# Attention of a decoder trunk on one Trainium2 core: one q/k/v projection per tile from strided views of h, and units that follow it by two steps

## What is computed

```
DILATION_PATTERNS = ((128, 1), (512, 4), (2048, 16))       # window, dilation
qkv = (x @ w_in).reshape(b, s, 3, N_GROUPS, ATTN_HEADS, ATTN_HEAD_DIM)
for g, (window, dilation) in enumerate(DILATION_PATTERNS):
    q = rms_norm(qkv[:, :, 0, g], q_gain[g]) * (ATTN_HEAD_DIM ** -0.5)
    k = rms_norm(qkv[:, :, 1, g], k_gain[g])
    o, l = dilated_window_attention(q, k, qkv[:, :, 2, g], rel_bias[:, g], window, dilation)
wts = jax.nn.softmax(jnp.stack(lses), axis=0)
y = jnp.einsum('gbsh,gbshe->bshe', wts, jnp.stack(outs))
```

## Time and profile before

| | before |
|---|---|
| median of 3 runs | 3387.8 us (3387.46 to 3390.41) |
| the profiled execution | 3383.74 us, its span 3382.0 us |
| granted clock, mean | 0.978 |
| busy: PE, PEld, DVE, ACT, POOL | 94%, 79%, 39%, 33%, 24% |
| attention, from first projection to last unit | 34.9 to 1301.6 us |

### The profile page before, as it was taken

One profiled execution on the slowest core, in us unless ns is written; L12 is line 12 of the kernel. 1 busy time (PEld: TensorE's weight loads), 2 busy tenths in 40 slices (PEclk: granted clock), 3 DMA queues, 4 the chain that ended last, 5 costly groups with the idle time before them and its releaser, 6 DMA issues. The chain is left out here.

```text
span 3382.0 us, 48256 instructions
## 1 busy us (share of the span) xinstructions
PE 3192.3 (94%) x17466; PEld 2669.5 (79%) x17466; DVE 1334.0 (39%) x3725; ACT 1102.1 (33%) x3002; POOL 825.2 (24%) x598
## 2 busy tenths in 40 slices
PE   4999999999999995999999999899877999999999
PEld 3888888888888883878888888678655788888887
DVE  6445454555555554341313133541064431313131
ACT  4555555555555553321111112210244211111020
POOL 3332333333233320212222122112111122222221
PEclk9999999999999995999999999999998999999999
DMA  2112121211112114111111111111201111111112
GB/s 98 36 40 59 41 58 40 61 49 50 52 45 53 47 32 150 50 44 47 48 50 44 50 50 45 38 44 50 81 26 57 44 50 44 50 50 44 50 45 80
DMA packets 89904, 177.01 MB, mean 52 GB/s; under 512 B 25515, under 2 KB 55870, under 8 KB 89662
## 3 DMA queue, kind: packets, MB, share of 16 engines
q1 hardware_dynamic: 87358, 169.63, 16.1%
q10 hardware_dynamic: 2304, 4.20, 0.3%
HBM read 160.67 MB, written 13.12 MB: 51 GB/s over the span
## 5 line engine op out<-in xcount | busy, mean ns | idle before, releaser
L69 PE MATMUL ps_qk<-w_hi,attn_hT_hi 128*128 128x256 f32 x1536 | 437.4, 285 | 23.3 <-DVE attn_hT_lo L213 9.7
L915 POOL TENSOR_TENSOR first_w_lo<-first_raw,first_w_hi 128x1024 fp32r<-128x1024 f32 x96 | 231.7, 2414 | 900.8 <-ACT first_w_hi L911 900.8
L70 PE MATMUL ps_qk<-w_lo,attn_hT_hi 128*128 128x256 f32 x1536 | 436.1, 284 | 0.0
L71 PE MATMUL ps_qk<-w_hi,attn_hT_lo 128*128 128x256 f32 x1536 | 436.1, 284 | 0.0
L857 POOL TENSOR_TENSOR w_lo<-raw,w_hi 128x384 fp32r<-128x384 f32 x192 | 194.6, 1015 | 701.9 <-ACT w_hi L602 701.9
L915 POOL TENSOR_TENSOR second_w_lo<-second_raw,second_w_hi 128x1024 fp32r<-128x1024 f32 x72 | 172.2, 2391 | 630.0 <-ACT second_w_hi L911 630.0
L69 PEld LDWEIGHTS ps_qk<-w_hi,attn_hT_hi 128*128 128x128 f32 x1536 | 294.1, 191 | 27.6 <-issue 13.3
L635 ACT ACTIVATE prob<-ps_s,neg_max 128x128 f32<-128x128 f32 (+1 forms) x384 | 156.6, 413 | 439.7 <-DVE neg_max L726 439.7
L70 PEld LDWEIGHTS ps_qk<-w_lo,attn_hT_hi 128*128 128x128 f32 x1536 | 294.7, 192 | 0.4
L71 PEld LDWEIGHTS ps_qk<-w_hi,attn_hT_lo 128*128 128x128 f32 x1536 | 294.9, 192 | 0.0
L69 PE MATMUL first_ps<-first_hid_hi,first_w_hi 128*128 128x512 f32 x640 | 255.4, 399 | 32.7 <-DVE first_hid_lo L1239 32.7
(11 more groups left out here) (276 smaller groups left out, 6853.9 us busy)
## 6 DMA issues: line engine op xcount, KB each, us to landing
raw<-in_wqkv SPq DMA_DIRECT2D x192, 192.0 KB, 2.3
first_raw<-in_w SPq DMA_DIRECT2D x64, 512.0 KB, 3.4
second_raw<-in_w SPq DMA_DIRECT2D x64, 512.0 KB, 3.4
w_bc<-share_dram SPq DMA_DIRECT2D x48, 256.0 KB, 4.2
first_raw<-in_vo_pieces SPq DMA_DIRECT2D x16, 512.0 KB, 3.5
bias<-bias_dram SPq DMA_DIRECT2D x16, 256.0 KB, 3.6
yT_dram<-o_g SPq DMA_DIRECT2D x8, 512.0 KB, 3.1
first_raw<-in_attn_wo SPq DMA_DIRECT2D x8, 512.0 KB, 3.5
```

The source lines that it names most:

```text
L69: pe.matmul(out, a_hi, b_hi, start=first, stop=False)
L70: pe.matmul(out, a_hi, b_lo, start=False, stop=False)
L71: return pe.matmul(out, a_lo, b_hi, start=False, stop=last)
L915: pool.tensor_tensor(self.lo[:, n % 2, :], self.raw[:, n % self.RAW, :], self.hi[:, n % 2, :].bitcast(F32), ALU.subtract).then_inc(self.lo ...
```

## The change

The q/k/v projection of a tile becomes one stream: 24 matmuls of 384 columns, `hT` stationary. The 128 tokens of a tile are now those of a unit, taken from h by a view: contiguous in group 0, every 4th token in group 1, every 8th in group 2 (`tile_view`). In group 2 a tile holds two residues modulo 16, and the bias masks the pairs that mix them (`bias_onehot`). q, k and v come out in the order that the units need, v with tokens in partitions, so the permuting copies, `vT` and its transposes are gone; `v_hi` holds 8 tiles. A unit starts two steps after its tile (`LAG = 2`), its weighted values two steps after its scores; the merge and the store follow about one superstep earlier, and supersteps run to 25.

```diff
+UNIT_STRIDE = (1, 4, 8)
...
+def tile_view(ap, g, u):
     if g == 0:
-        return ap
+        return ap[:, u * P:(u + 1) * P]
     if g == 1:
+        return ap.rearrange("p (n i r) -> p r n i", n=2, r=4)[:, u // 2, u % 2, :]
+    return ap.rearrange("p (m u) -> p u m", u=TT)[:, u, :]
...
-LAST_SUPER = SECTIONS + 2
+LAST_SUPER = SECTIONS + 1
+LAG = 2
...
-                U = T - TT
+                U = T - LAG
...
-                        mm = split_matmul(pe, ps_qk[j % 2][:, 0:2 * P],
-                                          hT_hi[:, k, j * P:(j + 1) * P], hT_lo[:, k, j * P:(j + 1) * P],
-                                          w_hi[:, par, k, 0:2 * P], w_lo[:, par, k, 0:2 * P], k == 0, k == KT - 1)
+                        mm = split_matmul(pe, ps_qkv[j % 2][:, 0:W3],
+                                          tile_view(hT_hi[:, k, :], st % NG, j), tile_view(hT_lo[:, k, :], st % NG, j),
+                                          w_hi[:, par, k, :], w_lo[:, par, k, :], k == 0, k == KT - 1)
...
+                if st < SECTIONS:
+                    if st >= 1 or j >= 2:
+                        pe.wait_ge(qkn_done, T - 1)
+                        pe.wait_ge(v_lo_done, T - 1)
+                    project(0, KT).then_inc(qkv_mm, 1)
+                if has_unit(st, j, 2):
+                    sec, u = unit(st, j, 2)
...
+                    for b in range(first, 2):
+                        slot = u - 1 + b
+                        mm = split_matmul(pe, ps_o[:, 0:2 * P], v_hi[:, slot, :], v_lo[:, slot, :],
+                                          pT_hi[:, b, :], pT_lo[:, b, :], b == first, b == 1)
...
-                    if st >= 1:
-                        if j == 0:
-                            pe.wait_ge(vT_done, 2 * N)
-                        mm = pe.transpose(ps_t[:, 2 * P:3 * P], vT[:, (st - 1) % 2, j * P:(j + 1) * P], ident[:])
...
-                    for k in range(2 * (j % 4), 2 * (j % 4) + 2):
-                        mm = split_matmul(pe, ps_v[:], w_hi[:, par, k, 2 * P:3 * P], w_lo[:, par, k, 2 * P:3 * P],
-                                          hT_hi[:, k, half * HALF:(half + 1) * HALF],
-                                          hT_lo[:, k, half * HALF:(half + 1) * HALF], k == 0, k == KT - 1)
...
-                    act.activation(sq[:], ps_qk[j % 2][:, 0:2 * P], ACT.Square).then_inc(squared, 1)
+                    act.activation(sq[:], ps_qkv[j % 2][:, 0:2 * P], ACT.Square).then_inc(squared, 1)
+                    act.copy(v_hi[:, j, :], ps_qkv[j % 2][:, 2 * P:W3]).then_inc(v_hi_done, 1)
...
-                if st >= 4 and (st - 4) % NG == 0:
-                    pair = (st - 4) // NG + 2 * i
+                if st >= 3 and (st - 3) % NG == 0:
+                    pair = (st - 3) // NG + 2 * i
```

More of the change, by code:

```diff
@@ L54, in bias_onehot @@
         band = window // dilation
+        mixed = dilation // UNIT_STRIDE[g]
         for x in range(BIAS_LEN):
-            step = x - (P - 1)
-            if step < 0 or step > band:
+            step, other = divmod(x - (P - 1), mixed)
+            if step < 0 or step > band or other:
                 out[g, REL_BUCKETS, x] = 1.0
@@ L349, in attention_phase @@
         gains = sb("gains", [P, 2, NG])
[L350 to L353, removed]
+        qk_hi = sb("qk_hi", [P, 2, SEQ], F32R)
+        qk_lo = sb("qk_lo", [P, 2, SEQ], F32R)
+        v_hi = sb("v_hi", [P, TT, P], F32R)
+        v_lo = sb("v_lo", [P, TT, P], F32R)
         sq = sb("sq", [P, 2 * P])
@@ L366, in attention_phase @@
         stat_rows = sb("stat_rows", [4 * TT, P])
-        vT, w_bc, prob = buffers.vT, buffers.w_bc, buffers.prob
+        w_bc, prob = buffers.w_bc, buffers.prob
         o_raw = [buffers.o_g0, total[:].rearrange("p (o t) -> p o t", o=1), buffers.o_g2]
         ring = sb("ring", [P, HALF])
[L370 to L379, removed]
+        compact = sb("compact", [P, NG, 2, 2, TT])
+        top = sb("top", [P, 2, TT])
+        diff = sb("diff", [P, NG, 2, TT])
+        grown = sb("grown", [P, NG, 2, TT])
+        part = sb("part", [P, NG, 2, TT])
+        den = sb("den", [P, 2, TT])
+        share = sb("share", [P, NG, 2, TT])
+        ps_qkv = [ps(f"ps_qkv{i}", [P, HALF]) for i in range(2)]
         ps_t = ps("ps_t", [P, HALF])
@@ L429, in _, with load_bias @@
             sp.dma_start(gains[HD:P, 1, :], k_gain).then_inc(gains_in, 16)
+            def load_bias(g, pair):
+                base = (g * HEADS + 2 * pair) * BIAS_LEN
+                width = 2 * P if g < 2 else P
+                sp.dma_start(bias[g][:], bass.AP(bias_dram.tensor, base, [[1, P], [BIAS_LEN, 2], [1, width]]))\
+                    .then_inc(bias_in[g], 16)
+            load_bias(0, 0)
             for n in range(TT + 4):
@@ L501, in step, with project @@
                 T = TT * N + j
-                U = T - TT
+                U = T - LAG
                 par = st % 2
[L504 to L508, removed]
+                def project(k_first, k_end):
+                    for k in range(k_first, k_end):
                         if st == 0 and j % 4 == 0:
@@ L575, in step @@
                         mm = split_matmul(pe, ps_s[h][:, c0:2 * P],
-                                          qk_hi[rows, sp_, 0, u * P:(u + 1) * P], qk_lo[rows, sp_, 0, u * P:(u + 1) * P],
-                                          qk_hi[rows, sp_, 1, k0:(u + 1) * P], qk_lo[rows, sp_, 1, k0:(u + 1) * P],
+                                          qk_hi[rows, 0, u * P:(u + 1) * P], qk_lo[rows, 0, u * P:(u + 1) * P],
+                                          qk_hi[rows, 1, k0:(u + 1) * P], qk_lo[rows, 1, k0:(u + 1) * P],
                                           True, True)
                     mm.then_inc(scored, 1)
[L580 to L584, removed]
-                    pe.wait_ge(p_hi_done, U)
-                    pe.wait_ge(p_lo_done, U)
-                    if has_unit(st, j, 2):
-                        pe.wait_ge(o_done, U - 1)
-                    first = 0 if has_prev(g, u) else 1
-                    for b in range(first, 2):
-                        slot = (whole - 1 + b) % 3
-                        mm = split_matmul(pe, ps_o[:, 0:2 * P], v_hi[:, slot, :], v_lo[:, slot, :],
-                                          pT_hi[:, b, :], pT_lo[:, b, :], b == first, b == 1)
-                    mm.then_inc(pv_done, 1)
             norm.sums(pe)
@@ L701, in _ @@
         def _(dve):
-            dve.memset(bias[2][64:P, :, 64:P], MASKED).then_inc(set_done, 1)
             dve.wait_ge(gains_in, 64)
@@ L768, in step @@
-                if j == 0:
-                    turned_tiles()
-                    turned_probabilities()
-                else:
-                    turned_probabilities()
-                    turned_tiles()
+                turned_probabilities()
+                if 1 <= TT * st + j <= TT * SECTIONS:
+                    dve.wait_ge(turn_hi, T)
+                    if j == 3 and st >= 1 and (st - 1) % NG < 2:
+                        if st >= 2:
+                            dve.wait_ge(rows_out, 16 * (2 * ((st - 1) // NG + 2 * i) + (st - 1) % NG))
+                        dve.tensor_copy(stat_rows[:], ps_t[0:4 * TT, 3 * P:4 * P]).then_inc(rows_done, 1)
+                    sec, t = divmod(TT * st + j - 1, TT)
+                    g = sec % NG
+                    for a in range(2):
+                        ins = dve.scalar_tensor_tensor(qk_lo[:, a, t * P:(t + 1) * P], ps_t[:, a * P:(a + 1) * P],
+                                                       gains[:, a, g:g + 1], qk_hi[:, a, t * P:(t + 1) * P].bitcast(F32),
+                                                       ALU.mult, ALU.subtract)
+                    ins.then_inc(turn_lo, 1)
@@ L824, in merge_step @@
                         ins.then_inc(share_done, 1)
-                    if j == 7:
-                        o0 = o_raw[0][:, ((st - 4) // NG) % 2, :]
+                if st >= 4 and (st - 4) % NG == 0:
+                    pair = (st - 4) // NG + 2 * i
+                    o0 = o_raw[0][:, ((st - 4) // NG) % 2, :]
+                    if j == 1:
                         dve.wait_ge(wbc_in[0], 64 * pair + 32)
```

227 lines of the change are left out of this document (81 added, 146 removed).

## The result

| | before | after |
|---|---|---|
| median | 3387.6 us (3386.6 to 3390.4) | 3532.6 us (3531.4 to 3533.7) |
| ratio, 95% interval | | 1.0427 [1.0409, 1.0445] |
| profiled span, granted clock | 3382.0, 0.978 | 3529.6, 0.977 |
| attention up to the first MLP matmul | 1332.5 | 1480.2 |

The kernel became 4.3% slower. The direction of the forecast held, and so did its mechanism, a weight load that pays for the stride. The size did not: its sum gave 3490 (3486, and 4 for the median), and the time lies 18 us above the upper end of its range, 3515.

The account below looks back on a forecast made before the run. TensorE, issuing without a gap, was taken as the bound. 3384 - 28 - 11 - 19 + 160 = 3486, plus 4 for the median gave 3490 us; the likeliest case's range was 3440 to 3515, the whole range starting at 3345.

Parts of the forecast that it names:

- Parts 1 and 2: Projection steps: one 384-column stream saves 0.04 us per step, dropping v's transpose 0.11; together -28 us.
- Part 3: Attention's units: lag 2 instead of 8 cuts the drain from 34.4 to about 12 us, adds 11 beside projections; net -11.
- Part 4: Waits between engines beside projections: values and scores wait for nothing; merge waits change by +18 us, or -19 with strided loads.
- Part 5: Projection in groups 1 and 2: a strided load of h takes 0.229 us, no longer hidden, costing +160 us.
- Rival 2: Projection's strided weight loads: a load just doubles, to 0.215; +117 us, time 3443; counted within the main mechanism (0.56).
- The loop's return: TensorE's waits where the loop returns: 6.0 us in two places, with no term for a change.

Follow-up runs that it names:

- experiment 1: The changed kernel with contiguous tiles of h in all groups (other tokens than groups 1 and 2 need): 3371.1 us, ratio 0.9954 to the kernel before.
- experiment 6: The changed kernel with 512 moving columns in 21 of the 24 projection matmuls, 128 more than needed: 3595.1 us.
- experiment 2: The changed kernel with h read at every second float in groups 1 and 2 (other tokens than needed): 3374.4 us, ratio 0.9965 to the kernel before.
- experiment 5: The kernel before, its 256-column q/k matmuls reading h at strides of 2, 3 and 6 floats in groups 0, 1 and 2: 3605.9 us.
- 4: The kernel before, its 256-column q/k projection reading h at strides of 7, 4 and 8 floats in groups 0, 1 and 2: 3868.9 us.
- experiment 7: The changed kernel with each projection matmul of 384 columns cut into three of 128: 5739.8 us.
- experiment 8: The changed kernel with 10 supersteps ahead of a loop of 2 rounds, so one loop return instead of two: 3526.4 us, ratio 1.0415 to the kernel before.

## Why the prediction was off

**Parts 1 and 2** held. Steps in group 0 without a wait take 5.66 and 6.28 to 6.31 us, predicted 5.71 and 6.34; with contiguous h the whole change gives 3371, predicted 3367. The pace at 384 columns is 0.174 and not 0.177, but the first of each projection is 0.28, and a projection comes to 4.28 where I had 4.25.

**Part 3** held in kind: the drain is 15.0, I had 12. Its rounds show why: transposes of prob begin at 1439.62, 1443.27 and 1446.56, each behind a wait for an exponential, so a round costs 3.3 to 3.6 as before, and the last one's values follow 2.2 us later.

**Part 4** held in kind. Values wait for nothing in the steady steps; waits for exponentials stand mostly around the merge. TensorE's waits beside projections, returns left out, were 22.5 us before. With free loads (experiment 1) they are 39.9, that is +17, predicted +18. With strided loads they are 15.2, that is -7, where the prediction had -19: the 1.5 us of room per step swallowed less than it assumed. The 41 us of experiment 1 are near its swing of 37 in part by luck, since some 5 of them are the clock, which it did not have.

**Part 5 is the step that failed, in its size.** It put a strided load at 229 ns and the cost at (0.229 - 0.177) x 3072 = 160 us. It measured 203, and that is the term of the sum that was mis-sized. The 43 us in four pieces, each from intervals above: the contiguous interval is 0.174, not 0.177 (+9); stride 4 has 0.2332 in 1472 intervals (+6); stride 8 has 0.2414 in 1472 (+18), where I had given both strides one price; and the first interval of each of 128 projections is dearer by 0.13 instead of 0.052 (+10), since behind the 64-row scores load and stream seem to add (experiment 6). The reason given, one piece of 16 bytes per 1.8 ns, was right: experiments 2 and 5 vary the number of pieces, 4, 6 and 7 the cover, and the interval is the longer of the two each time. Rival 2 (a load that doubles, to 0.215) falls with 0.2332, and with the 0.1735 of experiment 5.

**The loop's return** was counted as unchanged, at 6.0 us for the two gaps. By the steps it cost 7.9 before and 11.3 after, 3.4 more. Why the gap is longer was not settled. TensorE now waits for `qkn` and `v_lo` of the step just ahead. VectorE finished `v_lo` at 617.81, 2.0 ahead of the return's end, in the kernel after, and in experiment 8 the trace puts the gap that stayed down to `v_lo`. On the other hand the gaps were 3.2 and 3.0 in experiment 2 and 2.9 at the first return of experiment 6, with the same waits in the code, so the change does not always lengthen them. Nor does the length of the gap alone say what the clock does: it fell to 0.50 behind a gap of 3.0 at the second return before and in experiment 2, and stayed at 1.00 behind 3.0 at the first return before and 2.9 in experiment 6.

The 190 steps by these terms: 88 x 6.30 + 102 x 5.66 + 203 = 1334.7 and 34.8 of waits, against 88 x 6.34 + 102 x 5.71 + 160 = 1300 and 24 predicted. The steps are 9 us cheaper, the loads 43 dearer, and what is left 11 dearer: 3 of it the returns, the rest waits that did not shrink as much as predicted. With 3 in the drain and 3 less ahead of the first unit this is the miss, 45 us in the profiled execution and 43 in the medians. The range was too narrow on this side: it was meant to hold loads of 0.21 to 0.24, but 0.24 alone gives (0.24 - 0.177) x 3072 = 194 us in place of 160, some 3523, above its upper end.

## What to carry to other kernels

Before a strided fp32 view becomes a stationary operand, count the 16-byte pieces that its columns touch: at 1.8 to 1.9 ns each the load is hidden only if the matmul ahead of it is longer, and no other matmul's slack counts. Here 64 pieces (every second float) were free under 256 columns, 96 were not, and 128 needed about 512 columns above them. The order of work that the stride was meant to allow is worth 0.5%, but only with h stored so that the floats of a tile are contiguous or two apart. Storing h by residue modulo 4 would give group 1 contiguous tiles and group 2 a stride of two; group 0 would then need a second copy or a permuting pass. This was not built.

## What the runs showed of the hardware

- A strided 128-column weight load takes 0.2332 (every 4th float) to 0.2427 us (every 8th). For every 4th float it is the same under 384 and 256 moving columns at 2.4 GHz (0.2332, 0.2333) and under 128 at 1.2 GHz (0.2334), while a contiguous one under 128 columns goes from 0.1117 to 0.2133 with the clock. The Trainium skill (TensorE: Matmul & The Clock Gate, LDWEIGHTS) gives a load's time by its columns alone, columns / 1.2, which makes an estimate of 107 ns for 128. The contiguous rows at the full clock are within 5% of it; the strided ones show that the distance of the columns counts too.
- Every 8th float is dearer than every 4th, 6th or 7th (0.2414 against 0.2332, 0.2280, 0.235), and in the kernel after by 1% more for tiles 0 to 3 than for 4 to 7; in experiment 7, at the lower clock, all tiles had 0.2400. No run here explains it.
- The first matmul of 128 rows behind scores of 64 rows holds the next one back by 0.28 us with a contiguous load and 0.41 with a strided one at 384 columns, and by 0.06 more with 128 columns more.
- TensorE, busy for 148.00 of 148.00 us in the first stretch shown of experiment 7, had a granted clock of 0.50 there while it ran matmuls of 128 columns 0.24 us apart. In the kernel after it ran matmuls of 384 columns at the same distance with the clock at 1.00. No run here shows why.
- In experiment 1 the granted clock fell to 0.50 behind 4 of 11 waits of 1.9 to 2.0 us, and a projection there took up to 1.6 us more. No run here shows what sets those four apart.
